# Second mix: half of the gate projection behind the outputs' sums, spatial norm's weights and bias behind its product, keys' sum ahead of the reach

## The reference, cut to what matters

```python
h = modulate(rmsnorm(x, norm_mix[l]), sh1, sc1)
p = h @ w_in[l]                       # 5 * 512 + 2 * 512 columns: gates f, b; v; q; output gate; u; v of the MLP
# token_mixers
o_f, h_f = chunk_gla(q, k_f, v, logf_f, h0_f)           # forward and backward gated recurrences
o_b, h_b = chunk_gla(flip_t(q), flip_t(k_b), flip_t(v), flip_t(logf_b), h0_b)
o = rmsnorm(o_f + flip_t(o_b), hg_gain)                 # one norm for each of 4 heads of 128
o_hg = merge_heads(o) * silu(p[..., 4 * w:5 * w])       # the output gate
o_mlp = chunk_sgu(u, v, sgu_g, sgu_b, w_s, b_s)
x = x + g1 * (concatenate([o_hg, o_mlp]) @ w_out[l])

def chunk_sgu(u, v, ln_g, ln_b, w_s, b_s):              # chunks of 128 positions, 4 heads of 128 channels
    v = layernorm(gelu(v), ln_g, ln_b)
    z = einsum('hpq,bnqhc->bnphc', w_s, v) + b_s        # mixes the positions of a chunk
    return gelu(u) * z
```

## Time and profile before

| | us |
|---|---|
| median of 3 runs | 1399.5 |
| lowest, highest | 1395.93, 1400.88 |
| the profiled execution | 1391.34 |
| its span from first to last instruction | 1389.3 |

### The profile page before, as it was taken

How to read it: one execution, slowest core, us unless ns; L and a number is a source line. 1 busy time by engine, 2 the same in 40 slices (tenths; PEclk the granted TensorE clock), 3 DMA queues, 4 the chain that set the end, 5 groups by cost and what they waited for, 6 DMA issues and landing times.

```text
span 1389.3 us, 21888 instructions
## 1 busy us (share of the span) xinstructions
PE 1253.1 (90%) x9218; PEld 1165.7 (84%) x9218; DVE 937.6 (67%) x1294; ACT 634.1 (46%) x835; POOL 206.5 (15%) x139
## 2 busy tenths in 40 slices
PE   4998988989899999699878889999789887999995
PEld 3887878777899999696658888999789877999995
DVE  6767566554478874646864666874558835999994
ACT  4464343253543445555555565434433234544442
POOL 0000000000454441000000111210000002344431
PEclk9999999899899999899998999999899998999998
DMA  7441001001676654253223677875333213555530
GB/s 270 146 162 33 32 1 62 1 1 48 244 250 247 243 183 152 93 186 115 98 89 119 212 267 269 292 276 183 109 138 113 74 57 121 183 170 184 185 130 31
DMA packets 122656, 200.26 MB, mean 144 GB/s; under 512 B 3264, under 2 KB 111168, under 8 KB 112320
## 3 DMA queue, kind: packets, MB, share of 16 engines
q1 hardware_dynamic: 117664, 168.11, 35.8%
q0 software_dynamic: 3456, 25.17, 4.8%
q10 hardware_dynamic: 1440, 5.60, 1.1%
HBM read 197.82 MB, written 1.05 MB: 143 GB/s over the span
## 4 chain that ended last, share of the span: by engine, by line
PE 64%; DVE 24%; ACT 7%; issue 4%; DMA 0%; DVEq 0%; POOL 0%; ACTq 0%
PE bank L638 13%; PE bank L639 12%; PE bank L640 12%; DVE buf L2453 7%; DVE ring_r L1760 6%; PE bank L721 3%; PE bank L723 3%; PE bank L722 3%; ACT high L1211 3%; PE bank L901 2%; DVE work L2029 2%; PE bank L654 2%; DVE work L2025 2%; PE bank L889 2%; PE bank L1103 1%
## 5 line engine op out<-in xcount | busy, mean ns | idle before, releaser
L638 PE MATMUL bank<-part,high 128*128 128x256 f32 x1664 | 486.8, 293 | 58.9 <-DVE part L1767 51.1
L1760 DVE TENSOR_TENSOR ring_r<-ring,high 128x2048 fp32r<-128x2048 f32 (+1 forms) x155 | 343.8, 2227 | 205.8 <-ACT high L1211 203.5
L639 PE MATMUL bank<-part,high 128*128 128x256 f32 x1664 | 481.7, 290 | 0.0
L640 PE MATMUL bank<-part,ring_r 128*128 128x256 f32 x1664 | 481.2, 289 | 0.0
L638 PEld LDWEIGHTS bank<-part,high 128*128 128x128 f32 x1664 | 330.9, 199 | 66.0 <-issue 41.9
L639 PEld LDWEIGHTS bank<-part,high 128*128 128x128 f32 x1664 | 331.0, 199 | 1.3 <-issue 1.2
L640 PEld LDWEIGHTS bank<-part,ring_r 128*128 128x128 f32 x1664 | 330.7, 199 | 0.0
L1211 ACT ACTIVATE high<-ring 128x2048 fp32r<-128x2048 f32 x155 | 295.1, 1906 | 51.1 <-PE bank L640 40.9
L1687 POOL TENSOR_TENSOR ring_r<-ring,high 128x512 fp32r<-128x512 f32 x44 | 92.7, 2107 | 523.4 <-ACT high L1211 523.3
L721 PE MATMUL bank<-part,high 128*128 128x256 f32 x528 | 151.3, 286 | 9.2 <-POOL part L1681 4.9
L722 PE MATMUL bank<-part,high 128*128 128x256 f32 x528 | 150.1, 284 | 0.0
(11 more groups left out here) (267 smaller groups left out, 1568.5 us busy)
## 6 DMA issues: line engine op xcount, KB each, us to landing
ring<-in_wide SPq DMA_DIRECT2D x122, 1024.0 KB, 5.9
ring<-in_down SPq DMA_DIRECT2D x33, 1024.0 KB, 4.9
buf<-in_wide POOLq DMA_DIRECT2D x24, 1024.0 KB, 7.2
con<-in_cons SPq DMA_DIRECT2D x1, 1536.0 KB, 11.1
ring<-in_wide SPq DMA_DIRECT2D x2, 576.0 KB, 7.0
buf<-in_wide ACTq DMA_DIRECT2D x1, 1024.0 KB, 5.1
buf<-in_wide SPq DMA_DIRECT2D x1, 1024.0 KB, 5.2
buf<-in_ctx_t ACTq DMA_DIRECT2D x1, 1024.0 KB, 7.3
```

The source lines that it names most:

```text
L638: mm(bank, ah, bh, start=start, stop=False, skip_group_check=shared)
L639: mm(bank, ah, bl, start=False, stop=False, skip_group_check=shared)
L640: return mm(bank, al, bh, start=False, stop=stop, skip_group_check=shared)
L1760: v.tensor_tensor(low, raw, hi.bitcast(F32), ALU.subtract).then_inc(sem("unit_low"), 1)
```

## The change

Four edits, all but one in the second mix.

**Keys' sum.** On DVE `k_sum` (which lets PE start `diag`) is made ahead of the second product of `reach_q` instead of behind it.

**Spatial norm.** `values_normed` ends with the eight norming products; the two operations with weights and bias are gone. The weights come as columns (`sgu_g`, 4) into `spatial_out`, where the addition becomes a multiply and add with one operand from SBUF (`z_bias`). `z_bias` = rowsum(W) times the norm's bias (`sgu_b`, 4 columns) plus the position bias: PE makes the row sums with one product of ones and `wsp` (128x512, `wrow`) in `ffn(1)` behind `gate_up` of c = 9, and DVE four multiply and adds of 128 columns there. The rows' load shrinks from 768 to 256 KB, the columns' grows by 8 columns. `wrow` takes one turn of banks 4 to 7.

**Gate half.** `in_half(6, 1)` moves on PE from behind `cross` to behind `gsum`; `mo_half(2, 0)` from ahead of `gsum` to behind the upper halves 0 and 1. On ACT its Silu moves between the pieces 2 and 3, and the unit copy that waits for it behind piece 3; on DVE the split of that unit moves from behind the cross copies to behind the low piece 3, and the low piece 2 ahead of the gating of outputs 1.

**Low pieces.** On DVE the low pieces 0 and 1 of the mix go ahead of the last reach.

```diff
@@ PE, ffn(1)
+                    if c == 9:
+                        pe.wait_ge(sem("wsp_in"), 16)
+                        bank = open_bank(("wrow", 0))
+                        close(mm(bank[:, :], const("ones"), wsp, start=True, stop=True), ("wrow", 0))
@@ PE, second mix
                     close(last, ("cross", d))
-                in_half(6, 1)
                 mo_half(0, 0)
...
-                for i in range(1, MO_SPLIT):
-                    mo_half(i, 0)
+                mo_half(1, 0)
                 for j in range(2):
                     pe.wait_ge(sem("go_sq"), j + 1)
...
-                for i in range(MO_SPLIT):
+                in_half(6, 1)
+                for i in (0, 1):
                     mo_half(i, 1)
-                mo_half(3, 0)
-                mo_half(3, 1)
+                for i in (2, 3):
+                    mo_half(i, 0)
+                    mo_half(i, 1)
@@ ACT, behind rsqrt_of
                 part_of("mix", 2)
+                key = ("in", 6, 1)
+                wait_full(eng, key)
+                release(act_(piece(gate_x, 1), bank_of(key)[:, :], ACT.Silu), key)
                 part_of("mix", 3)
+                ahead("in", 6, 1)
@@ DVE, ffn(1)
+                    if c == 9:
+                        key = ("wrow", 0)
+                        wait_full(eng, key)
+                        eng.wait_ge(sem("rows_in"), 16)
+                        for h in range(HG):
+                            one = slice(h * P, (h + 1) * P)
+                            ins = v.scalar_tensor_tensor(z_bias[:, one], bank_of(key)[:, one], pcol("sgu_b", h), prow("b_spatial")[:, one], ALU.mult, ALU.add)
+                            own.go(ins) if h < HG - 1 else release(ins, key)
@@ DVE, second mix
+                    if d == 2:
+                        v.tensor_tensor(k_sum, reach_k[:, 0:4, :], reach_k[:, 4:8, :], ALU.add).then_inc(sem("diag_ready"), 1)
                     four = slice(4 * d - 4, 4 * d)
...
-                v.tensor_tensor(k_sum, reach_k[:, 0:4, :], reach_k[:, 4:8, :], ALU.add).then_inc(sem("diag_ready"), 1)
...
-                        own.go(v.tensor_scalar(z, z, bna[:, i, 0:1], bna[:, i, 1:2], ALU.subtract, ALU.mult))
-                    own.settle()
-                    eng.wait_ge(sem("rows_in"), 16)
-                    own.step(v.tensor_tensor(vv_x, vv_x, spread(prow("sgu_g"), [P, TT, 512]), ALU.mult))
-                    v.tensor_tensor(vv_x, vv_x, spread(prow("sgu_b"), [P, TT, 512]), ALU.add).then_inc(sem("vv_ready"), 1)
+                        ins = v.tensor_scalar(z, z, bna[:, i, 0:1], bna[:, i, 1:2], ALU.subtract, ALU.mult)
+                        own.go(ins) if i < 7 else ins.then_inc(sem("vv_ready"), 1)
...
-                            ins = v.tensor_tensor(dst, bank_of(key)[:, i * S:(i + 1) * S].rearrange("p (t n) -> p t n", t=TT),
-                                                  spread(prow("b_spatial")[:, h * P:(h + 1) * P], [P, TT, P]), ALU.add)
+                            ins = v.scalar_tensor_tensor(dst, bank_of(key)[:, i * S:(i + 1) * S].rearrange("p (t n) -> p t n", t=TT), pcol("sgu_g", h),
+                                                         spread(z_bias[:, h * P:(h + 1) * P], [P, TT, P]), ALU.mult, ALU.add)
```

38 lines of the change are left out of this document (20 added, 18 removed).

## The result

| | before | changed |
|---|---|---|
| median of the runs, us | 1400.19 (4 runs, 1395.93 to 1401.15) | 1380.49 (4 runs, 1378.16 to 1387.23) |
| profiled execution, us | 1391.34 | 1379.04 |
| its span, us | 1389.3 | 1377.1 |
| mean granted clock | 0.953 | 0.953 |

The ratio is 0.9873, interval 0.9832 to 0.9914: by it 17.8 us faster (12.0 to 23.5), where 9.3 were forecast. (The two medians lie 19.7 apart; each is of four runs that scatter by 5 to 9 us. The profiled executions differ by 12.3 only. That gap between 12.3 and 17.8 is the first thing to explain, the other is why even 12.3 is more than 9.3.

What follows compares the result with a forecast made beforehand. PE's standstills in the second mix, each followed by half clock, and the DVE and ACT relay at its end were taken as the bound; +0.9 - 2.2 - 5.1 - 2.2 + 0.2 - 0.9 = -9.3 us gave 1390.2, range 1385 to 1397.

Steps and rivals of the forecast that it cites:

- row sums' product: In ffn(1), one added fp32 product of 128x512 on PE, paid in full: +0.9 us, bounds 0.4 to 2.7.
- Nothing here depends on which: Starting time: the forecast starts from the runs' median 1399.5, not the profiled 1391.34, claiming the choice doesn't matter.
- keys' sum: Second mix, before diag: PE starts 1.15 us earlier and the half clock behind is shorter, -2.2 us.
- values' norm: Before the spatial product: 2.5 us less waiting and the clock stays up after a 1.9 us standstill, -5.1 us.
- cross to sums of squares: Gate half and low pieces: new 3.9 us standstill behind cross, half clock costing 2.65, yet -2.2 us.
- relay's start: Output end of the second mix: DVE's first residual starts 0.2 us later counted from the sums of squares, +0.2.
- norm's last records: End of the mix: PE waits 1.8 us, the clock stays, last four records take 1.2 not 2.08: -0.9 us.
- The 2.31 row: Profile row used for the keys' sum: a 2.31 us standstill brought the clock down for 3.4 us only.
- The clock falls all the same: Rival: the shortened standstills still drop PE's clock, so only waiting counts: -4.8 us, 1394.7, chance 0.2.
- DVE bounds the levels: Rival: DVE, later than reckoned, holds PE at cross and the position bias is unhidden: -3.1 us, 1396.4, chance 0.12.
- No fall at the short handovers: Rival: neither the 2.5 nor the 3.9 us standstill brings the clock down: -13.1 us, 1386.4, chance 0.1.
- The ring holds the relay: Rival: a ring slot freed 20 us later delays feed forward 2's units; 1406.4 at 30 us landing, chance 0.04.

Runs made afterwards that it cites:

- a1_after_oldplaces: Changed kernel with the 8 new columns in a tile behind all others, so every other tile lies as before: 1380.33 us, ratio 0.9896 of before.
- p4_pad256: Kernel before with con and all tiles behind it 256 bytes further: 1400.76 us, one run.
- n1_norm_only: Kernel before with only the spatial norm edit, new columns in a tile behind all others: 1393.11 us, ratio 0.9986.
- k1: Kernel before with only the keys' sum moved ahead of the second reach product: 1393.34 us, one run.
- v1_both_192: Changed kernel with unit copy ahead of the square and gate half cut in two, con and behind 192 B further than before: 1361.12 us, ratio 0.9769.
- v2_both_224: Changed kernel with unit copy ahead of the square and gate half cut in two, con and behind 224 B further than before: 1376.5 us, ratio 0.9858.
- a0: The changed kernel run again, unaltered: 1375.49 us, ratio 0.9872 of before.
- c1: Changed kernel with ACT's unit copy ahead of the square of the residual: 1380.29 us, ratio 0.9889 of before.
- h1: Changed kernel with unit copy ahead of the square, gate half cut in two, outputs 0 squared before outputs 1 are copied: 1374.81 us, ratio 0.9854 of before.
- l1: Changed kernel with low pieces 0 and 1 put back behind the last reach: 1387.76 us, one run.
- g1: Kernel before with only the gate half and low pieces edits, all tiles as before: 1391.34 us, ratio 0.9968.

## Why the prediction was wrong in size and mostly right in its steps

**The step that failed** is a term that the prediction put at nothing without a reason: the change section says that the columns' table grows by 8 columns, and the sum has no price for that. It moves all buffers by 64 B against the weights, and PE's products start every 117.8 ns instead of 120.0. Ahead of the mix that gives 6.5 us, which with the row sums' product (0.86) makes the 5.7 between 984.46 and 990.12, at equal half clock. Alone the 8 columns gave a ratio of 0.9954. Without them the edits give nearly the same stage (a1_after_oldplaces) and nothing ahead of it. With -5.7 ahead of the stage in place of +0.9, the sum would have been -15.9; the stage gave 1.9 more than the forecast's 10.2 (0.5 of it by the pace, 0.9 by the mis-sized term below, 0.4 by a shorter half clock at the stage's start, little in the others) and the part behind it 0.4, which makes 18.2.

**"Nothing here depends on which"** execution was the second mistake, in two ways. First, the start: 1399.5 was the median of three runs of a kernel whose median in 63 later executions is 1395.3. Of the 9.7 us between the forecast's 1390.2 and the measured 1380.5, 4.2 is this. From 1395.3 the same sum gives 1386.0. (The changed kernel's four runs drew high as well: its median was 1375.5 when it ran again.) The ratio, at nearly twice the forecast, owes nothing to this. Second, the profiled execution of before had a clock of 1.00 at 303 to 322, and that of the changed kernel 0.73, so their difference was not that of the runs. Where the half clock there is 10.2 us instead of none (and 3.4 us longer at 250 in the same executions), the mix starts 5.3 us later (990.12 and 995.46; 984.46 and 989.78), and where it is 23.9 us 9.5 later (999.58 in p4_pad256, whose pace is that of before). That fits the levels of 1391, 1396 and 1401 and their mean clocks.

The terms, by the marks of a1_after_oldplaces against before, where the pace is the same:

| term | forecast | measured | from |
|---|---|---|---|
| row sums' product | +0.9 | +0.86 | 944.15 to 945.13, less 0.12 |
| half clock at the stage's start | none | -0.4 | diag: -1.54, of which 1.15 is the wait; the same -0.4 in n1_norm_only |
| keys' sum | -2.2 | -2.3 to -2.5 | 1.15, and 1.17 (k1) to 1.34 behind it |
| values' norm | -5.1 | -4.9; -3.3 where the clock fell | wait 4.40 to 1.87; spatial product to cross 19.15 to 16.76 |
| cross to sums of squares | -2.2 | -3.1 | 23.08 to 19.98 |
| relay's start | +0.2 | +0.2 | 31.32 to 31.53 |
| norm's last records | -0.9 | -0.9 | 7.51 to 6.57 |

**Row sums.** Right: 0.86, as read off the four records of the earlier trace rows. DVE's four operations took 1.12 of at most 1.8 and hid.

**Keys' sum.** Right: 2.53 of wait, and 3.4 us of half clock in seven of the nine executions of the changed order (in v1_both_192 and v2_both_224 the clock stayed). The 2.31 row was the right neighbour. That the old wait fell for 6.8 us was not certain, though: it did in nine of eleven.

**Values' norm.** DVE ready at 1.87 us after PE, as forecast (1.9). "Stays at 1.9" was right in five of the seven executions with this wait at the old or the 64 B places (a0, a1, c1, h1, l1; window 1078.30 above) and wrong in two, the profiled one of the changed kernel and n1_norm_only. It stayed as well behind the 1.87 and 1.74 us of v2_both_224 and v1_both_192. Nothing that was varied here tells the cases apart, so this term is worth 4.9 or 3.3, and that the clock stayed in most is not something that one row of 1.93 could promise. What was to be late next, the reach ahead of cross, wasn't: no wait for it anywhere.

**Gate half and low pieces.** The standstill behind cross is 3.82 (forecast 3.9). The half clock behind it was sized from the earlier trace rows at 5.3 us and lasted 3.4 in every execution (a0, a1, c1, g1, and the profiled one), so the step cost 1.7 and not 2.65, and the sums of squares came 19.9 us behind cross's start instead of the forecast's 20.9. This is the mis-sized term: 0.9. Its bound of -4.2 for no fall is also off: 1118.0 + 6.7 + 2.9 is 1127.6, 4.5 before 1132.1; no other number but that rival's sum hangs on it. The chain behind came out to 0.1 us on ACT and DVE (Silu G+8.8, residual G+14.26) and to 0.3 in PE's waits: 1.4 for piece 3 (forecast 1.7), 2.1 at the norm (forecast 1.8), where the clock stayed for the four records, 1.13 (forecast 1.2).

The Trainium skill, "ScalarE: Activation LUTs", section "What ACT_TABLE_LOAD costs", would have put Silu 1.4 us later. The trace differs: ACT's copy of piece 2 ended at 1128.00, the new load began at 1128.02 and took 1.28 us, and Silu started at 1129.31, so no drain of 1.38 stands on either side. The row held.

**The rivals.** "The clock falls all the same" came true at the norm in two executions, at diag and cross for 3.4 us, and never as a whole. "DVE bounds the levels" didn't happen. "No fall at the short handovers" happened at diag in the two kernels at 192 and 224 B only. "The ring holds the relay" didn't: ACT waits there only for DVE and PE, never for a unit.

What stays open: why the distance of operands sets PE's pace, why 192 B is best of those tried and 224 hardly helps, why the ring's place changes the pace of products that don't read it, and what decides in the first block's stage at 310 us whether the clock falls.

## What to carry over

Count a change of a table's size as an edit: see which tiles it moves against each other, and when a time differs by more than the path can give, compare the pace of PE's stream far from the edit before looking for a reason near it. Compare profiled executions at equal half clock, and check a stage that wasn't changed first, since here one such stage is worth 5 to 10 us from run to run. Take the starting time from more than three runs where the scatter is as wide as the gain. A standstill's price has two parts, and the second (3.4, 6.8 or 10.2 us of half clock) is better read from several executions than from the nearest row of one.

## What the hardware showed

- The start to start time of the 128x256 passes of split products at full clock depended on the distance between weights and activations in a partition: 120.0 ns with 0 and 256 B added, 117.0 with 32, 117.6 with 64, 119.0 with 128, 114.6 with 192, 118.4 with 224. Moving all tiles together by 64 B left it at 120.0. Moving the ring alone by 64 B changed it to 115.8 ns where the weights come from the ring and to 118.9 where they don't. In whole kernels: 0.9954 for the 64 B alone, 1374.81 to 1361.12 us from 64 to 192 B (in part by a higher mean clock).
- A standstill of 1.9 us brought the clock to 0.50 for 3.4 us in two of seven executions with the same work around it; one of 2.5 us did in seven of nine (not in the two at 192 and 224 B). One of 3.7 us did in all eleven, for 6.8 us in nine and 3.4 in two; one of 3.8 in another place in all five, for 3.4 us; the one of 5.3 for 6.8.
- One fp32 product of 128x512 in a stream of 128x256 passes put the stream off by 0.86 us (two records, 0.43 apart). The record of the product behind it began 0.46 after its start and was 0.68 long in place of 0.28.
